# Small parameter loads on three DMA queues, the eleventh input-projection tile split earlier on ScalarE, and the latent norms moved ahead in a hybrid RG-LRU / MLA layer

## The chip, the cores and the metric

The kernel runs on one core of one Trainium2 chip. The metric is the device time of one execution in microseconds, and lower is better. TensorE (PE) does the matmuls, VectorE (DVE) and ScalarE (ACT) the elementwise work, GpSimd (POOL) some of it too, and SyncE (SP) only issues DMAs. ACT and POOL can issue DMAs as well.

## The reference

One layer with two kinds of sequences: a prompt of 512 tokens, and 8 sequences that decode one token each against 4096 cached tokens. So T = 520 columns pass through every projection.

```python
mod = jnp.dot(jax.nn.silu(c), lp['w_ada']) + lp['b_ada']
shift1, scale1, gate1, shift2, scale2, gate2 = jnp.split(mod[:, None, :], 6, axis=-1)
h = rms_norm(x, lp['norm1_g']) * (1.0 + scale1) + shift1
z = h @ lp['w_in']
x_lru, g_lru, q_lat, kv_lat, k_rope = jnp.split(z, IN_SPLITS, axis=-1)
x_conv, lru_buf_new = causal_dwconv(x_lru, ...)
hs, h_last = rg_lru(x_conv, pos, lru_h0, ...)          # h_t = a_t h_(t-1) + u_t, a = exp(log_a)
lru_out = hs * jax.nn.gelu(g_lru)
q = rms_norm(q_lat, lp['q_lora_norm_g']) @ lp['w_uq']   # then norms and rotary embedding
kv_lat = rms_norm(kv_lat, lp['kv_lora_norm_g'])
k_rope = apply_rope(rms_norm(k_rope, lp['k_rope_norm_g']), cos, sin)
attn = attend(q_nope, q_rope, kv_lat, k_rope)
mixed = concat(rms_norm(lru_out), rms_norm(attn)) @ lp['w_o']
x = x + gate1 * mixed
...                                                     # norm, up projection, convolution, gelu, down projection
```

All is fp32. A matmul of weight precision is done as three products of a high and a low part.

## The kernel before

Data lie transposed: 128 features on the partitions, 520 tokens in the free dimension. Each engine has its own program, written out by hand and run strictly in order; semaphores tie them together.

**The start.** SP loads constants, the conditions c, the prompt x in two halves of 1 MB, and then the chunks of `w_ada` (1 MB each, 24 in all) into a ring of four. Chunk 4 may only be loaded when PE has used chunk 0, and so on (`chunk_used`). ACT meanwhile issues 25 small loads: rows of parameters into `par_rows`, the states, and four copies of the page table into `page_of` (L1308 to L1326). Only then comes its first activation, the tanh behind silu(c) (L1329), from which DVE makes `cT` (L1681, L1682). PE turns c (J_C, PSUM buffer 0), then the eight tiles of x (J_XT), the fourth of which needs buffer 0 back from DVE. Then PE multiplies `cT` with the first two chunks of `w_ada` (L866), turns the parameter rows (it waits for all 21 loads counted by `s_par`), and goes on with chunks 2 and 3. The eight columns of shift and scale that come out of the first eight chunks are needed before the input projection can begin.

**The input projection.** `w_in` has 12 column tiles, taken in the order `WIN_ORDER`; `w_in(n)` is the n-th of them on PE (48 matmuls of 260 columns). Its weights pass through three stages: SP loads them, ACT rounds them to their high part (`in_high(n)`, L1342, which must wait until tile n - 2 is through PE, since `input_weights` has two buffers), and POOL makes the low part (`in_low(n)`, L732). Tiles 0 to 3 are the recurrent branch, 4 to 7 the latents of q, kv and the rotary key (`latent`, L1362), 8 to 11 the gate branch; the latter are copied out of PSUM on ACT by `gate_branch(0)` to `gate_branch(3)` (L1393). Between the tiles PE computes later chunks of `w_ada` (L866), turns their results (`mod_columns`), and makes the sums of squares for three norms (`nq`, `nkv`, `kr0`). Between the copies ACT computes the recurrence's coefficients: four Exp (L1385) and four Tanh (L1388), then two Ln (L1400, L1401) and an Exp (L1406), and the reciprocal roots of the three norms (`rstd`, L1297 and L1299). DVE does the scan (L1809) and multiplies the norms in (L1817, L1819, L1823).

**PSUM.** There are four buffers of two banks. Every piece of PE work has a number j and uses buffer j mod 4. It may start (`claim`) only when the piece with number j - 4 has been copied out. `IN_ORDER` is the list that gives the numbers in this stretch, and the programs of all engines follow them:

```python
def claim(eng, j, lap=0):
    if j // 4 >= 1 or not isinstance(lap, int):
        eng.wait_ge(psum_free[j % 4], j // 4 + lap)
```

After it come the small outputs of the recurrence, eight heads of prompt attention, the decode attention over the cache, and the MLP.

Of the kernel before, what the change touches and what calls it, by code (L numbers as in the profile page):

```python
# [111 lines left out]
class Steps:  # L112
# [20 lines left out]
    def leave(self, laps):  # L133
# [18 lines left out]
            + ["w6", "r4", "w7", "c3", "w8", "w9", "nq", "nkv", "kr0", "r5", "w10", "c4", "w11", "kr1", "c5"])  # L152
# [105 lines left out]
def build(nc, t):  # L258
    with ExitStack() as ctx:
# [308 lines left out]
        def _(sp):  # L568
# [30 lines left out]
            for c in range(8):  # L599
                if c >= 4:  # L600
                    chunk_used(sp, c - 4)
                modulation(c, c % 4, s_ada[c % 4])
                if c == 5:
                    w_in(0)
                    w_in(1)
# [226 lines left out]
        def _(pe):  # L832
# [135 lines left out]
            w_in(9)  # L968
# [8 lines left out]
            both(j, C("blk", QK, R)[:, NOPE:QK], sq[NOPE:QK, 3, :], True, True, R).then_inc(psum_full[j % 4], 1)  # L977
            later_chunk(12)
# [309 lines left out]
        def _(act):  # L1288
# [19 lines left out]
            for name in ("b_ada", "norm1_g", "lru_conv_b", "lru_b_a", "lru_b_x", "lru_lambda",  # L1308
                         "q_lora_norm_g", "kv_lora_norm_g", "lru_out_norm_g", "mla_out_norm_g", "norm2_g"):
                load_rows(name, t[name].rearrange("l (r p) -> (l r) p", p=P))  # L1310

            load_rows("lru_conv_w", t["lru_conv_w"].rearrange("l w (r p) -> (l w r) p", p=P))
            for name, a, b in (("gq", "q_nope_norm_g", "q_rope_norm_g"), ("gk", "k_nope_norm_g", "k_rope_norm_g")):
                r = ROWS[name]
                act.dma_start(par_rows[r:r + 1, 0, 0:NOPE], t[a]).then_inc(s_par, 16)
                act.dma_start(par_rows[r:r + 1, 0, NOPE:QK], t[b]).then_inc(s_par, 16)
            fw = t["ffn_conv_w"].rearrange("l w (r p) -> (l w r) p", p=P)
            act.dma_start(par_rows[0:4 * FT, 1, :], fw[0:4 * FT, :]).then_inc(s_par, 16)
            act.dma_start(par_rows[0:2 * FT, 2, :], fw[4 * FT:6 * FT, :]).then_inc(s_par, 16)
            act.dma_start(par_rows[2 * FT:4 * FT, 2, :],  # L1320
                         t["ffn_conv_b"].rearrange("l (r p) -> (l r) p", p=P)).then_inc(s_par, 16)
            act.dma_start(st_tok, t["state_lru_conv"].rearrange("l b r w -> (l b r) w")).then_inc(s_par, 16)
            act.dma_start(h0_tok, t["state_lru_h"].rearrange("l b w -> (l b) w")).then_inc(s_par, 16)

            for r in range(4):
                act.dma_start(page_of[r:P:4, :], t["page_table"].rearrange("b n -> n b"), allow_slow_non_contiguous=True).then_inc(s_pt, 16)  # L1326
# [55 lines left out]
            in_high(9)  # L1382

# [267 lines left out]
        def _(dve):  # L1651
# [163 lines left out]
            dve.wait_ge(s_rs, 2)  # L1815
            for k in range(2):
                V.scalar_tensor_tensor(qlT[:, k, :], qlT[:, k, :], pr("q_lora_norm_g", k), sq[:, 0, :], MUL, MUL).then_inc(s_ql, 1)  # L1817
            dve.wait_ge(s_rs, 3)
            V.scalar_tensor_tensor(kvT[:, :], kvT[:, :], pr("kv_lora_norm_g"), sq[:, 1, :], MUL, MUL).then_inc(s_kvn, 1)  # L1819
# [387 lines left out]
```

## Time and profile before

| | |
|---|---|
| median of 3 runs | 1120.18 us (1119.37 to 1123.1) |
| the profiled execution: its time | 1124.76 us |
| the profiled execution: its span in the trace | 1123.0 us |
| mean granted TensorE clock | 0.937 of full speed |
| PE busy | 1005.5 us, 90% of the span |
| DVE, ACT, POOL busy | 671.2, 537.9, 196.8 us |
| DMA | 100.28 MB, mean 89 GB/s |

PE is busy nine tenths of the span, and 70% of the chain that ended last is PE's. The 1.76 us between the span and the execution's time lie outside the trace. Everything in this case happens in the first 165 us: the start up to about 55 us, and the input projection up to about 150 us.

### The profile page before, as it was taken

What the parts mean: (1) busy time and instruction counts of PE and PEld (TensorE: products, weight loads), DVE (VectorE), ACT (ScalarE), POOL (GpSimd) and SP (SyncE); (2) the same over time, 40 slices, a digit from 0 to 9 for tenths busy, and PEclk for the clock granted to TensorE, in tenths of its full rate; (3) what the DMA queues carried; (4) which work ended last, traced back from release to release, by engine and by line L of the source; (5) the groups of instructions that cost most, each with busy time, mean ns of one, the idle gap of its engine ahead of it and who ended that gap; (6) DMA issues with size and microseconds to landing.
All of it is one profiled execution on the core that took longest, in us unless ns stands there. A gap on an engine that the chain in (4) does not pass through costs nothing.

```text
span 1123.0 us, 21332 instructions
## 1 busy us (share of the span) xinstructions
PE 1005.5 (90%) x7916; PEld 904.9 (81%) x7916; DVE 671.2 (60%) x1553; ACT 537.9 (48%) x875; POOL 196.8 (18%) x202
## 2 busy tenths in 40 slices
PE   6699989999797977978978699799999999999997
PEld 4388755444496977977878689699999999999997
DVE  4591356656676657567557545667777777753212
ACT  3314736555487758658658443344444434322210
POOL 0233231000123422432432202211000010100000
PEclk9699987988899999899899879899999999999999
DMA  8975534000100211211201014222423233263202
GB/s 292 303 244 180 187 117 156 13 10 2 49 18 20 95 50 45 93 34 60 92 21 56 1 38 132 51 76 75 112 75 110 77 94 93 81 177 91 71 3 77
DMA packets 110527, 100.28 MB, mean 89 GB/s; under 512 B 10451, under 2 KB 99454, under 8 KB 108381
## 3 DMA queue, kind: packets, MB, share of 16 engines
q1 hardware_dynamic: 105478, 78.36, 23.5%
q0 software_dynamic: 3456, 20.97, 5.3%
q8 instruction: 36, 0.59, 0.2%
q10 hardware_dynamic: 1539, 0.22, 0.1%
q14 instruction: 18, 0.15, 0.0%
HBM read 96.80 MB, written 2.94 MB: 89 GB/s over the span
## 4 chain that ended last, share of the span: by engine, by line
PE 70%; DVE 9%; ACT 8%; issue 8%; POOL 2%; DMA 1%; ACTq 1%; DVEq 0%; POOLq 0%; SPq 0%
PE ps L841 46%; PE ps L1174 12%; PE ps L836 4%; PE ps L1078 2%; PE ps L866 2%; POOL latents_low L795 2%; DMA RW<-w_ada 1%; PE ps L1134 1%; DVE RB L2009 1%; ACT RB L1528 1%; DVE RB L1893 1%; ACT RB L1512 1%; PE ps L1169 1%; PE ps L1042 1%; PE ps L1059 1%
## 5 line engine op out<-in xcount | busy, mean ns | idle before, releaser
L841 PE MATMUL ps<-normed_high,up_weights_high 128*128 128x260 f32 x704 | 142.7, 284 | 3.6 <-DVE normed_low L1728 3.4
L841 PE MATMUL ps<-normed_high,up_weights_low 128*128 128x260 f32 x704 | 142.3, 284 | 0.0
L841 PE MATMUL ps<-normed_low,up_weights_high 128*128 128x260 f32 x704 | 142.1, 284 | 0.0
L795 POOL TENSOR_TENSOR latents_low<-RB,latents_high 128x512 fp32r<-128x512 f32 (+1 forms) x72 | 86.1, 1202 | 274.6 <-ACT latents_high L1513 224.6
L1174 PE MATMUL ps<-key_weights_high,latents_high 128*128 128x260 f32 x528 | 120.7, 312 | 13.0 <-DVE RB L2007 11.8
L841 PEld LDWEIGHTS ps<-normed_high,up_weights_high 128*128 128x128 f32 x704 | 109.2, 190 | 4.3 <-issue 3.5
L1174 PE MATMUL ps<-key_weights_low,latents_high 128*128 128x260 f32 x528 | 111.4, 294 | 0.0
L1575 ACT ACTIVATE up_weights_high<-RW 128x1024 fp32r<-128x1024 f32 x44 | 46.6, 1060 | 135.4 <-PE ps L841 132.9
L1174 PE MATMUL ps<-key_weights_high,latents_low 128*128 128x260 f32 x528 | 111.3, 294 | 0.0
L841 PEld LDWEIGHTS ps<-normed_high,up_weights_low 128*128 128x128 f32 x704 | 109.0, 189 | 0.0
L841 PEld LDWEIGHTS ps<-normed_low,up_weights_high 128*128 128x128 f32 x704 | 108.8, 189 | 0.0
L1174 PEld LDWEIGHTS ps<-key_weights_high,latents_high 128*128 128x128 f32 x528 | 87.2, 204 | 16.7 <-DVE RB L2007 14.7
L1174 PEld LDWEIGHTS ps<-key_weights_high,latents_low 128*128 128x128 f32 x528 | 86.8, 201 | 0.0
L1174 PEld LDWEIGHTS ps<-key_weights_low,latents_high 128*128 128x128 f32 x528 | 86.8, 201 | 0.0
L2088 DVE TENSOR_TENSOR up_weights_low<-RW,up_weights_high 128x1024 fp32r<-128x1024 f32 x44 | 54.9, 1251 | 34.3 <-ACT up_weights_high L1575 29.9
L1528 ACT ACTIVATE qrot<-ps 128x512 f32<-128x512 f32 x88 | 52.9, 601 | 45.4 <-PE ps L1174 41.7
L841 PE MATMUL ps<-hidden_high,down_weights_high 128*128 128x260 f32 x352 | 71.4, 284 | 1.3 <-issue 1.3
L2006 DVE COPY RB<-ps 128x32 f32<-128x32 f32 (+1 forms) x72 | 13.6, 188 | 96.1 <-ACT qrot L1528 52.4
L841 PE MATMUL ps<-hidden_high,down_weights_low 128*128 128x260 f32 x352 | 70.8, 282 | 0.0
L841 PE MATMUL ps<-hidden_low,down_weights_high 128*128 128x260 f32 x352 | 70.7, 282 | 0.0
L2077 DVE TENSOR_TENSOR d<-ps,modT 128x8 f32<-128x8 f32 x16 | 2.7, 166 | 107.8 <-PE ps L841 107.8
L828 POOL COPY UT<-RW 128x10 f32 x44 | 24.8, 563 | 238.9 <-ACT RW L1601 238.9
(282 smaller groups left out, 2268.4 us busy)
## 6 DMA issues: line engine op xcount, KB each, us to landing
RW<-w_ada SPq DMA_DIRECT2D x24, 1024.0 KB, 7.9
RW<-w_up SPq DMA_DIRECT2D x44, 512.0 KB, 5.0
RW<-w_down SPq DMA_DIRECT2D x8, 1408.0 KB, 7.1
RW<-w_in SPq DMA_DIRECT2D x11, 512.0 KB, 8.3
RB<-w_o SPq DMA_DIRECT2D x8, 512.0 KB, 4.7
RB<-x_prompt SPq DMA_DIRECT2D x2, 1024.0 KB, 7.1
o_y_p<-RB SPq DMA_DIRECT2D x4, 512.0 KB
wuq<-w_uq SPq DMA_DIRECT2D x8, 96.0 KB, 2.1
```

Source lines behind the costliest of these rows:

```text
L795: nc.gpsimd.tensor_tensor(latL[:, g % 3, c:4 * P], turned[:, g % 3, c:4 * P], latH[:, g % 3, c:4 * P].bitcast(F32), ALU.subtract).then_inc ...
L828: nc.gpsimd.tensor_copy(UT[:, bass.ds(FT * g + 2 * i + e, 1), :], UU[e][:, g, NP:UW]).then_inc(s_ut, 1)
L836: return nc.tensor.transpose(out, in_, ident[0:n, 0:n])
L841: last = mm(ps[j % 4][rows[0]:rows[1], h, 0:H], lhsT, src[:, h * H:(h + 1) * H], start=start, stop=stop)
L866: last = mm(flat(j)[32 * g:32 * g + 32, 0:256], cT[:, k, :], ring[:, q if n < 2 else q % 2, kk, 256 * g:256 * g + 256], start=(k == 0), st ...
L1042: last = mm(flat(J.vw[e])[:, VD * a:VD * a + VD], kvT[:, P * a:P * a + P], wukv[:, e, NOPE:P], start=True, stop=True)
L1078: last = mm(flat(J.pv[e])[VD * e:VD * e + VD, P * a:NP], hb[e]["v"][:, VD * a:VD * a + VD], hb[e]["pt"][:, a, P * a:NP], start=(a == 0), s ...
L1174: last = mm(ps[j % 4][:, h, 0:KWW], a[:, g % 3, at:at + P], b[:, e, h, :], start=(i == 0), stop=(i == 2))
L1528: A(sqd[c % 3].rearrange("p (h n) -> p h n", h=2), ps[j % 4][:, :, 0:4 * NOPE], ACT.Square).then_inc(s_sqd, 1)
L1575: A(wuH[:, KT * g:KT * g + KT, :], wup[:, c, KT * g:KT * g + KT, :], ACT.Copy).then_inc(s_whi, 1)
L2006: V.tensor_copy(srd[e][:, HEADS * c:HEADS * c + w], flat(j)[:, KWW:KWW + w]).then_inc(s_snc, 1)
L2088: V.tensor_tensor(wuL[:, KT * g:KT * g + KT, :], wup[:, c, KT * g:KT * g + KT, :], wuH[:, KT * g:KT * g + KT, :].bitcast(F32), SUB).then_i ...
```

## The change

It has three parts. (1) Of ACT's 25 small loads six stay on ACT. Fifteen go to SP, behind the first four chunks of `w_ada` and ahead of the fifth. The four of the page table go to POOL. (2) `in_high(10)` on ACT moves ahead of the four Exp and four Tanh of the recurrence. (3) The sums of squares for the q, kv and rotary-key norms move ahead of `w_in(9)` on PE, their roots on ACT ahead of `gate_branch(0)`, and the two multiplications of q and kv on DVE ahead of the recurrence's tail; on DVE `mod_columns(3)` and `mod_rows(4)` move ahead of the wait for the Tanh. The job numbers follow by `IN_ORDER`.

```diff
-            + ["w6", "r4", "w7", "c3", "w8", "w9", "nq", "nkv", "kr0", "r5", "w10", "c4", "w11", "kr1", "c5"])
+            + ["w6", "r4", "w7", "c3", "w8", "nq", "nkv", "kr0", "w9", "r5", "w10", "c4", "w11", "kr1", "c5"])
...
-            for c in range(8):
-                if c >= 4:
-                    chunk_used(sp, c - 4)
+            for c in range(4):
+                modulation(c, c, s_ada[c])
+            sp.wait_ge(s_parz, 1)
...
+            for name in ("q_lora_norm_g", "kv_lora_norm_g", "lru_out_norm_g", "mla_out_norm_g", "norm2_g"):
+                load_rows(name, t[name].rearrange("l (r p) -> (l r) p", p=P))
...
+            sp.dma_start(h0_tok, t["state_lru_h"].rearrange("l b w -> (l b) w")).then_inc(s_par, 16)
+
+            for c in range(4, 8):
+                chunk_used(sp, c - 4)
                 modulation(c, c % 4, s_ada[c % 4])
...
             nc.gpsimd.memset(BD[:, :, :, :], 0.0).then_inc(s_bdz, 1)
+            for r in range(4):
+                nc.gpsimd.dma_start(page_of[r:P:4, :], t["page_table"].rearrange("b n -> n b"), allow_slow_non_contiguous=True).then_inc(s_pt, 16)
...
             w_in(8)
             later_chunk(11)
-            w_in(9)
             norm_sum(J_NQ, 2, KT)
             norm_sum(J_NKV, 1, KT + 2, 2)
...
+            w_in(9)
             later_chunk(12)
...
             latent(11, krT[NOPE:QK, :])
             in_high(9)
+            in_high(10)
 
             for k in range(LT):
                 v = st.did(A(AA[:, k, :], TA[:, k, :], ACT.Exp, bias=small[:, 32 + k:33 + k], scale=small[:, 32 + k:33 + k]))
...
             nc.scalar.preload_act_table_set("natural_log_exp_and_others")
+            rstd(J_NQ, QL, dst=sq[:, 0, :]).then_inc(s_rs, 1)
+            rstd(J_NKV, KV, dst=sq[:, 1, :]).then_inc(s_rs, 1)
+            rstd(J_KR[0], 1, (NOPE, QK), dst=sq[NOPE:QK, 2, :]).then_inc(s_rs, 1)
             gate_branch(0)
-            in_high(10)
...
+            mod_columns(3)
+            mod_rows(4)
             dve.wait_ge(s_ta, 4)
             V.tensor_scalar(TA[:, :, :], TA[:, :, :], 1e-18, None, ALU.max).then_inc(s_tiny, 1)
-            mod_columns(3)
-            mod_rows(4)
+            dve.wait_ge(s_rs, 2)
+            for k in range(2):
+                V.scalar_tensor_tensor(qlT[:, k, :], qlT[:, k, :], pr("q_lora_norm_g", k), sq[:, 0, :], MUL, MUL).then_inc(s_ql, 1)
```

On ACT, before, from `in_high(9)` on, which follows the copy of the last latent tile; L1385 and L1388 are the Exp and Tanh of the recurrence, L1393 is `gate_branch`, L1342 is `in_high`:

```order
L1342 ACTIVATE input_weights_high<-RW 128x1024 [waits psum_full0,w_in_in0]
L1385 ACTIVATE RB<-RB,small 128x520 x4
L1388 ACTIVATE RB<-RB,small 128x520 [waits act_steps]
L1388 ACTIVATE RB<-RB,small 128x520 x3
L1395 ACT_TABLE_LOAD
L1393 ACTIVATE RB<-ps 128x520 [waits psum_full2]
L1342 ACTIVATE input_weights_high<-RW 128x1024 [waits psum_full2,w_in_in1]
```

And now, from `in_high(10)` on, which follows `in_high(9)` directly (line numbers are those of the changed kernel: L1349 is `in_high`, L1393 and L1396 are Exp and Tanh, L1321 and L1323 the roots of the norms, L1401 `gate_branch`):

```order
L1349 ACTIVATE input_weights_high<-RW 128x1024 [waits psum_full2,w_in_in1]
L1393 ACTIVATE RB<-RB,small 128x520 x4
L1396 ACTIVATE RB<-RB,small 128x520 [waits act_steps]
L1396 ACTIVATE RB<-RB,small 128x520 x3
L1403 ACT_TABLE_LOAD
L1321 ACTIVATE sq<-ps,small 128x520 [waits psum_full3]
L1323 ACTIVATE sq<-sq 128x520 [waits psum_free3]
L1321 ACTIVATE sq<-ps,small 128x520 [waits psum_full0]
L1323 ACTIVATE sq<-sq 128x520 [waits psum_free0]
L1321 ACTIVATE sq<-ps,small 32x520 [waits psum_full1]
L1323 ACTIVATE sq<-sq 32x520 [waits psum_free1]
L1401 ACTIVATE RB<-ps 128x520 [waits psum_full2]
```

The L1349 of tile 10, which waits for tile 8 to be through PE (`psum_full2`), now stands ahead of the eight Exp and Tanh, and six operations of the norms stand between the table load and the copy of tile 8.

On PE, before, from the last matmuls of tile 8 (buffer `ps2`) to the first of tile 9:

```order
L841 MATMUL ps2<-normed_high_59,input_weights_low_65 128x260 x2
L866 MATMUL ps3<-RW,cT 32x256 [waits w_ada_second_in1]
L866 MATMUL ps3<-RW,cT 32x256 x7
L841 MATMUL ps3<-normed_high_59,input_weights_high_64 128x260 [waits input_weights_low,psum_free3]
L841 MATMUL ps3<-normed_high_59,input_weights_high_64 128x260
```

And now:

```order
L865 MATMUL ps2<-normed_high_59,input_weights_low_65 128x260 x2
L890 MATMUL ps3<-RW,cT 32x256 [waits w_ada_second_in1]
L890 MATMUL ps3<-RW,cT 32x256 x7
L865 MATMUL ps3<-sq,cst 128x260 [waits squares_done,psum_free3]
L865 MATMUL ps3<-sq,cst 128x260
L865 MATMUL ps3<-sq,cst 128x260 [waits squares_done]
L865 MATMUL ps3<-sq,cst 128x260
L865 MATMUL ps0<-sq,cst 128x260 [waits squares_done,psum_free0]
L865 MATMUL ps0<-sq,cst 128x260
L865 MATMUL ps1<-sq,cst 32x260 [waits squares_done,psum_free1,other_consts_in]
L865 MATMUL ps1<-sq,cst 32x260
L865 MATMUL ps2<-normed_high_59,input_weights_high_64 128x260 [waits input_weights_low,psum_free2]
```

The norms' sums take buffers 3, 0 and 1, and tile 9 now takes buffer 2, which is tile 8's; before it took buffer 3, that of the `w_ada` row ahead of it.

## Rows read from the trace of the kernel before

**Rows 1.** The page: shares of the chain of work that ended last.

```profile
PE 70%; DVE 9%; ACT 8%; issue 8%; POOL 2%; DMA 1%; ACTq 1%; DVEq 0%; POOLq 0%; SPq 0%
```

**Rows 2.** The chain of waits, first 60 us: start, duration, engine and line.

```profile
12.27 1.28 ACT L1329
...
22.51 6.30 DMA RW<-w_ada
```

**Rows 3.** The timeline of PE and ACT in the first 24 us.

```profile
4.40 0.99 PE L836 MATMUL ps<-cst,RB 9*128 9x9 f32 x8 [4.40 <-DMA RB<-x_sample]
8.17 3.81 PE L836 MATMUL ps<-cst,RB 128*128 128x128 f32 x15 [2.78 <-DMA RB<-x_prompt]
14.48 6.30 PE L836 MATMUL ps<-cst,RB 128*128 128x128 f32 x25 [2.50 <-DVE cT L1682]
20.71 2.60 PE L866 MATMUL ps<-RW,cT 128*32 128x256 f32 x32
...
3.64 0.38 ACTq L1306 DMA_DIRECT2D par_rows<-q_lora_norm_g  x1
...
9.19 0.32 ACTq L1323 DMA_DIRECT2D RB<-state_lru_h  x1
```

**Rows 4.** DMA queues and rate in the first 60 us (40 slices of 1.5 us).

```profile
GB/s 0 139 124 393 396 401 392 403 378 386 318 391 383 323 45 63 284 369 363 358 335 298 374 401 415 421 377 323 376 415 407 291 195 273 267 62 0 0 87 330
...
q10 hardware_dynamic: 1539, 0.22, 2.4%
```

**Rows 5.** Timelines: SP's issues of transfers, POOL's first split, DVE's reading of the page table.

```profile
4.61 1.50 SPq L583 DMA_DIRECT2D RW<-w_ada  x2
...
27.43 4.28 SPq L583 DMA_DIRECT2D RW<-w_ada  x2
...
34.45 4.66 POOL L732 TENSOR_TENSOR input_weights_low<-RW,input_weights_high 128x1024 fp32r<-128x1024 f32 x2 [32.41 <-ACT input_weights_high L1342]
...
93.83 0.22 DVE L1788 TENSOR_SCALAR row_of<-page_of,cst 128x8 int32<-128x8 int32 x1
```

**Rows 6.** PE's timeline around tiles 8 and 9 and the norms' sums.

```profile
122.85 0.40 PE L841 MATMUL ps<-normed_high,input_weights_low 128*128 128x260 f32 x2
123.18 1.07 PE L866 MATMUL ps<-RW,cT 128*32 128x256 f32 x16
124.99 0.51 PE L841 MATMUL ps<-normed_high,input_weights_high 128*128 128x260 f32 x2 [0.74 <-DVE newrow L1664]
...
130.85 3.78 PE L841 MATMUL ps<-sq,cst 128*128 128x260 f32 x16
134.56 1.93 PE L866 MATMUL ps<-RW,cT 128*32 128x256 f32 x32
```

**Rows 7.** ACT's timeline in the same stretch.

```profile
116.19 1.06 ACT L1342 ACTIVATE input_weights_high<-RW 128x1024 fp32r<-128x1024 f32 x1
117.15 2.95 ACT L1385 ACTIVATE RB<-RB,small 128x520 f32<-128x520 f32 x4
...
123.11 1.28 ACT L1395 ACT_TABLE_LOAD   x1
124.41 0.60 ACT L1393 ACTIVATE RB<-ps 128x520 f32<-128x520 f32 x1
...
134.32 0.69 ACT L1297 ACTIVATE sq<-ps,small 128x520 f32<-128x520 f32 x1
...
137.68 0.63 ACT L1299 ACTIVATE sq<-sq 32x520 f32<-32x520 f32 x1
```

**Rows 8.** DVE's timeline: its wait for the last `w_ada` row.

```profile
150.70 0.42 DVE L1664 COPY newrow<-ps 128x256 f32<-128x256 f32 x1 [5.32 <-PE ps L866]
```

**Rows 9.** PE's timeline after a wait of 5.14 us, in the decode attention.

```profile
407.67 0.53 PE L1169 MATMUL ps<-QBD,RB 128*128 x2 [5.14 <-POOL latents_low L795]
408.02 0.78 PE L1174 MATMUL ps<-key_weights_high,latents_high 128*128 128x260 f32 x2
...
411.20 0.42 PE L1174 MATMUL ps<-key_weights_low,latents_high 128*128 128x260 f32 x2
```

More of the change, by code:

```diff
@@ L597, in w_in, with load_rows @@
                 sp.dma_start(RA[:, n % 3, :, at:at + w], wi[:, :, P * m:P * m + w]).then_inc(s_win[n % 3], 16)
-            for c in range(8):
-                if c >= 4:
-                    chunk_used(sp, c - 4)
+            for c in range(4):
+                modulation(c, c, s_ada[c])
+            sp.wait_ge(s_parz, 1)
+            def load_rows(name, src):
+                n = src.shape[0]
+                sp.dma_start(par_rows[ROWS[name]:ROWS[name] + n, 0, 0:src.shape[1]], src).then_inc(s_par, 16)
+            for name in ("q_lora_norm_g", "kv_lora_norm_g", "lru_out_norm_g", "mla_out_norm_g", "norm2_g"):
+                load_rows(name, t[name].rearrange("l (r p) -> (l r) p", p=P))
+            load_rows("lru_conv_w", t["lru_conv_w"].rearrange("l w (r p) -> (l w r) p", p=P))
+            for name, a, b in (("gq", "q_nope_norm_g", "q_rope_norm_g"), ("gk", "k_nope_norm_g", "k_rope_norm_g")):
+                r = ROWS[name]
+                sp.dma_start(par_rows[r:r + 1, 0, 0:NOPE], t[a]).then_inc(s_par, 16)
+                sp.dma_start(par_rows[r:r + 1, 0, NOPE:QK], t[b]).then_inc(s_par, 16)
+            fw = t["ffn_conv_w"].rearrange("l w (r p) -> (l w r) p", p=P)
+            sp.dma_start(par_rows[0:4 * FT, 1, :], fw[0:4 * FT, :]).then_inc(s_par, 16)
+            sp.dma_start(par_rows[0:2 * FT, 2, :], fw[4 * FT:6 * FT, :]).then_inc(s_par, 16)
+            sp.dma_start(par_rows[2 * FT:4 * FT, 2, :],
+                         t["ffn_conv_b"].rearrange("l (r p) -> (l r) p", p=P)).then_inc(s_par, 16)
+            sp.dma_start(st_tok, t["state_lru_conv"].rearrange("l b r w -> (l b r) w")).then_inc(s_par, 16)
+            sp.dma_start(h0_tok, t["state_lru_h"].rearrange("l b w -> (l b) w")).then_inc(s_par, 16)
+            for c in range(4, 8):
+                chunk_used(sp, c - 4)
                 modulation(c, c % 4, s_ada[c % 4])
@@ L1306, in load_rows @@
                 act.dma_start(par_rows[ROWS[name]:ROWS[name] + n, part, 0:src.shape[1]], src).then_inc(s_par, 16)
-            for name in ("b_ada", "norm1_g", "lru_conv_b", "lru_b_a", "lru_b_x", "lru_lambda",
-                         "q_lora_norm_g", "kv_lora_norm_g", "lru_out_norm_g", "mla_out_norm_g", "norm2_g"):
+            for name in ("b_ada", "norm1_g", "lru_conv_b", "lru_b_a", "lru_b_x", "lru_lambda"):
                 load_rows(name, t[name].rearrange("l (r p) -> (l r) p", p=P))
[L1312 to L1326, printed above, removed]
             full(act, J_C)
@@ L1406, in _ @@
             A(TA[:, :, :], TA[:, :, :], ACT.Exp, scale=0.5).then_inc(s_lru, 1)
-            rstd(J_NQ, QL, dst=sq[:, 0, :]).then_inc(s_rs, 1)
-            rstd(J_NKV, KV, dst=sq[:, 1, :]).then_inc(s_rs, 1)
-            rstd(J_KR[0], 1, (NOPE, QK), dst=sq[NOPE:QK, 2, :]).then_inc(s_rs, 1)
             gate_branch(2)
@@ L1797, in _ @@
             v = st.did(V.scalar_tensor_tensor(TI[:, :, :], TI[:, :, :], 1.0, XC[:, :, :], ADD, MUL))
+            mod_columns(3)
+            mod_rows(4)
             dve.wait_ge(s_ta, 4)
             V.tensor_scalar(TA[:, :, :], TA[:, :, :], 1e-18, None, ALU.max).then_inc(s_tiny, 1)
-            mod_columns(3)
-            mod_rows(4)
+            dve.wait_ge(s_rs, 2)
+            for k in range(2):
+                V.scalar_tensor_tensor(qlT[:, k, :], qlT[:, k, :], pr("q_lora_norm_g", k), sq[:, 0, :], MUL, MUL).then_inc(s_ql, 1)
+            dve.wait_ge(s_rs, 3)
+            V.scalar_tensor_tensor(kvT[:, :], kvT[:, :], pr("kv_lora_norm_g"), sq[:, 1, :], MUL, MUL).then_inc(s_kvn, 1)
             dve.wait_ge(s_lru, 1)
@@ L1813, in _ @@
             dve.wait_ge(s_lrud, 1)
[L1815 to L1819, printed above, removed]
             dve.wait_ge(s_rs, 4)
```

## The prediction

> **What bounds the kernel now.** I read the page first: the chain that ended last is 70% PE [rows 1], so a change pays where PE waits. Then the chain of waits over the first 60 us, the timelines of PE, ACT and SP beside it and the DMA rates by slice, for the small loads. Then PE's, ACT's and DVE's timelines from 115 to 155 us, for the other two parts, and last a place in the decode stage where PE works after a long wait, for the clock.
>
> At the start ACT issues loads until its first table load at 12.27 us [rows 2], and PE, which had turned the first three tiles of x by 11.98, waits 2.50 us for what DVE makes of ACT's tanh [rows 3]. PE then reaches the first `w_ada` chunk at 20.71 us, and only when that is used does SP issue chunk 4, at 22.51. In between the DMA engines run dry: 45 and 63 GB/s in the two slices from 21 to 24 us, between slices of 323 and 284 [rows 4]. From there the chain runs through DMA: the load issued at 22.51 takes 6.30 us to land [rows 2]. So this stage goes as early as chunk 4 is issued.
>
> In the input projection PE is the bound. Tile 8 ends at 122.85 + 0.40 = 123.25 us, and tile 9 starts at 124.99 after a wait of only 0.74 [rows 6]. ACT uses exactly the time in which PE does tile 8 for the recurrence: Exp and Tanh from 117.15 until the table load at 123.11, and at 124.41 it copies tile 8 out [rows 7]. That ordering is what the change touches.
>
> **Part 1, the small loads.** ACT's sixth load is issued before the seventh begins at 3.64 us, and the turned c is ready at 4.40 + 0.99 = 5.39 [rows 3]. With the table load of 1.28 us [rows 2] done by 4.9, the tanh can run at about 5.4 and `cT` is there before 6.5, so PE isn't stopped: 3.81 + 6.30 = 10.11 us of turning from 8.17 ends at 18.28 in place of 20.71 [rows 3]. That is 2.43 us. The second half of x and chunk 0 have to be there: at the rates of rows 4, the 2.3 MB of constants, c and x have passed by about 9.3 us, chunk 0 by about 12, and chunk 3 by about 20.4. Chunk 4 is then issued at about 20.1, and the dry stretch shrinks by as much. All that follows in this stage keeps its distance to chunk 4, until PE-bound work begins at about 55 us. Gain: 2.4 us.
>
> What the moved loads cost: fifteen issues on SP, 0.39 us each if they are like ACT's (3.64 to 9.19 + 0.32 = 9.51, fifteen issues [rows 3]), begin at 4.61 + 1.50 = 6.1 us, when chunk 3 has been issued [rows 5], and end at about 12, well before 20.1; SP is waiting there anyway. They stand ahead of chunk 4 in SP's queue. All 1539 packets of ACT's queue, of which the page table is 1024, took 2.4% of 60 us, 1.4 us [rows 4]; so the delay of chunk 4 is between 0 and 1.4 us, and nearer to 0, since it falls into what remains of the dry stretch. The page table is read at 93.83 us; on POOL its four issues stand in front of nothing until 34.45 [rows 5]. Bounds for part 1: gain 1.0 to 2.4.
>
> **Parts 2 and 3, on ACT and PE.** These must be costed together, since the price comes from PSUM. `w_in(9)` now takes tile 8's buffer, which `gate_branch(0)` frees. So tile 9 can't start before ACT has copied tile 8, and ACT has put everything else first. From tile 8's end at 123.25, in the times of before [rows 7]:
>
> - `in_high(10)`: it waits for that end itself. 1.06 us
> - four Exp, four Tanh: they stood under tile 8, and now start after it. From 116.19 + 1.06 = 117.25 to 123.11: 5.86 us
> - table load with its gap, 123.11 to 124.41: 1.30 us
> - three norm roots, from 134.32 to 137.68 + 0.63 = 138.31: 3.99 us
> - the copy of tile 8: 0.60 us
>
> The sum is 12.81 us, and tile 9 starts at 136.1 in place of 124.99, 11.1 later. The norms' sums have meanwhile been done, from about 124.8 (chunk 11 ends at 124.25, and DVE copies a row in 0.42 [rows 8]). Between tile 9 and chunk 12 they took 134.56 - 130.85 = 3.71 us [rows 6]. Net: 11.1 - 3.7 = 7.4 us later, in which PE has nothing at all to do from about 128.5 to 136.1.
>
> Is any of it hidden further on? The moved multiplications on DVE give nothing: DVE had finished its work at 145.4 and sat idle for 5.32 us before 150.70, waiting for PE [rows 8]. Nor do they hold anything up: with the Exp and Tanh 7 us late, Ln, Ln, Exp and the scan follow, and by their durations before, DVE is through with `krT` about 3 us before it is needed. The later tiles keep their distances. The earlier split of tile 10 gives nothing either: in_low(10) had no one waiting for it. From 151 us on the chain passes from PE to DVE, ACT and POOL without a reserve that could absorb a delay.
>
> **The clock.** After a wait of 5.14 us PE's pairs of matmuls from 408.02 to 411.20 took 3.18 us for seven steps [rows 9], where tile 9 makes its 24 steps in 130.85 - 124.99 = 5.86 us, 0.244 each [rows 6], so 1.71 for seven. The new wait is longer, 7.6 us, with little work on either side of it left out. I take the same loss: 1.5 us. Bounds: 0 (PE keeps its higher level, 2.4 GHz) and 1.5.
>
> **The sum.** -2.4 + 7.4 + 1.5 = +6.5 us. Against the profiled execution, 1124.76 us, that is 1131.3. That execution stands 4.6 us above the median of the runs, 1120.18; the predicted median is 1126.7.
>
> **The rivals.**
> 1. *The start gives nothing, or costs* (0.14). SP's queue accepts only so much ahead: two `w_ada` issues that began at 27.43 took 4.28 us [rows 5], when much was outstanding. If the fifteen small loads are held until chunk 3 is through at 20.4, their 5.9 us of issuing push chunk 4 from 20.1 to 26.3, 3.8 us later than before. Or the parameters land late: PE needs them at about 21 us, before chunk 2. No row of before shows when they land. If they come with chunk 3 plus one transfer's latency, at 22 to 23 us, PE loses 1 to 2 us there, but chunk 6, which waits for chunk 2, was issued only from 27.43 [rows 5], so about 2 us of cover remain. The result is between +8.9 (no gain) and +12.7 us: 1129 to 1133. Against it: before, SP had issued x and four chunks by 6.1 us without such a delay [rows 5].
> 2. *The wait is partly absorbed* (0.10). If the clock stays up and ACT's list is shorter than I count, because the roots of the norms start only with their sums or the pipelined Exp overlap more, the loss is 5 us and the net +2 to +3: 1122 to 1123.5, within the measurement. For it speaks only that neighbouring ACT instructions overlap by 0.1 us (116.19 + 1.06 against 117.15 [rows 7]).
> 3. *Faster* (0.06). Tile 9 is not held by tile 8's copy, because ACT reaches it in time: then only the start's 2.4 us and tile 9's 0.74 us remain, 1117.0. This case decides when the copy ends before 124.99 + 3.71 + 2.4 = 131.1 us in before's times, that is when ACT's list of 12.8 us takes under 7.8. The eight Exp and Tanh alone are 5.9 of it, and the two waits on buffer 2 are in the program's order; so its chance is small. It is also the case where the change's second part does not reach the path.
>
> **How the numbers follow.** Forecast 0.70, with a range of its own of 1124 to 1129 (clock loss 0 to 1.5, start 1.0 to 2.4, and a median of three that varies by 1 to 2 us). Rival 1 takes 0.14, rival 2 0.10, rival 3 0.06. The range of 1123 to 1131 holds the forecast's and parts of rivals 1 and 2. A difference of 0.3%, 3.4 us, is about what a measurement of this kernel can tell from none. The forecast and rival 1 are slower by more, 0.84, and a little of rival 2; most of rival 2 and half of rival 3 lie within it, half of rival 3 below.
>
> **What would show it.** PE's first table-dependent wait (2.50 us for `cT`) gone, chunk 0 on PE at 18.3 us, chunk 4 issued at about 20.1, and tile 0 starting about 2.4 us earlier. Then PE idle for about 7.6 us in front of the first matmul of `w_in(9)`, put down to ACT's copy (L1401), ACT idle from about 115 to 121 us and full after that, and some 3 us of matmuls at the lower granted clock behind it. The end of tile 11 some 6.5 us later. I am wrong if that wait is short, if the parameters hold PE for more than 2 us, or if the stages after 165 us change by more than 1 us.

## The result, and the profile of the changed kernel

| | median | single runs |
|---|---|---|
| changed kernel | 1131.11 us | 1126.37 to 1136.23, 9 runs |
| kernel before, in turn with it | 1123.1 us | 1119.37 to 1126.61, 9 runs |
| ratio | 1.0073 | 95% interval 1.0045 to 1.0101 |
| profiled execution: its time and span | 1130.16 and 1128.4 us | clock 0.936 |

The change makes the kernel slower by 8.0 us. The forecast was slower, 1126.7 us, in a range of 1123 to 1131; the median lies 0.1 us above that range. The kernel before also stands 2.9 us above the median that the forecast started from: its nine runs contain the three of that median and six more.

The chain of work on the page of the changed kernel, against [rows 1]: PE's share fell from 70% to 68%, and DMA's rose from 1% to 2%.

```profile
PE 68%; DVE 10%; ACT 9%; issue 8%; POOL 2%; DMA 2%; SPq 1%; ACTq 0%; DVEq 0%; POOLq 0%
```

PE's timeline from the start, against [rows 3] (start, duration, engine and line, operation, count, and in brackets the idle time with what ended it):

```profile
8.04 10.04 PE L860 MATMUL ps<-cst,RB 128*128 128x128 f32 x40 [2.47 <-DMA RB<-x_prompt]
18.01 3.63 PE L890 MATMUL ps<-RW,cT 128*32 128x256 f32 x32
25.15 0.71 PE L860 MATMUL ps<-cst,par_rows 109*128 109x109 f32 x3 [3.51 <-DMA RB<-state_lru_h]
...
...
38.49 1.93 PE L890 MATMUL ps<-RW,cT 128*32 128x256 f32 x16 [0.61 <-DMA RW<-w_ada]
41.29 0.66 PE L860 MATMUL ps<-cst,newrow 128*128 128x128 f32 x2 [0.86 <-DVE newrow L1671]
```

The last two rows are chunk 7, the last that the input projection waits for, and what PE does with the row that DVE copies from it. In the kernel before they read:

```profile
40.21 1.93 PE L866 MATMUL ps<-RW,cT 128*32 128x256 f32 x16 [0.62 <-DMA RW<-w_ada]
42.78 0.66 PE L836 MATMUL ps<-cst,newrow 128*128 128x128 f32 x2 [0.64 <-DVE newrow L1664]
```

The wait of 2.50 us for `cT` is gone. A wait of 3.51 us for the last small load, `state_lru_h`, stands 7 us later. SP's timeline shows where that load stands, and that chunk 4 goes out at 20.00 us, where before had 22.51:

```profile
3.21 2.92 SPq L583 DMA_DIRECT2D RW<-w_ada  x4
6.18 1.53 SPq L605 DMA_DIRECT2D par_rows<-q_lora_norm_g  x1
...
14.17 0.58 SPq L620 DMA_DIRECT2D RB<-state_lru_h  x1
20.00 2.10 SPq L583 DMA_DIRECT2D RW<-w_ada  x2
```

In the chain of waits it takes 10.84 us from issue to landing, behind the four chunks of 1 MB, and DVE's products with `rs`, which follow the late norm sum, are on the chain with 9.21 us:

```profile
14.17 10.84 DMA RB<-state_lru_h
...
30.06 0.70 ACT rs L1321
30.79 0.65 ACT rs L1323
31.46 9.21 DVE RB L1714 x8
...
40.81 0.35 DVE newrow L1671
```

In the kernel before the same eight products took 4.91 us:

```profile
28.08 4.91 DVE L1707 TENSOR_TENSOR RB<-xT,rs 128x512 f32<-128x512 f32 x8 [0.17 <-ACT rs L1299]
```

The rates of the first 60 us, against [rows 4], in slices of 1.5 us: the dry stretch of 45 and 63 GB/s is gone, and a hollow of 264, 260 and 139 GB/s stands at 6 to 10.5 us, after POOL's four page-table issues at 2.00 us. GpSimd's queue is the third row.

```profile
GB/s 0 120 134 398 264 260 139 414 418 421 410 415 407 404 340 320 377 393 373 308 307 394 410 405 433 352 330 394 407 408 228 204 240 262 51 0 0 79 319 382
...
q0 software_dynamic: 128, 0.00, 2.0%
```

PE's timeline of the input projection, against [rows 6]: the norm sums at 122.99 us, then 7.47 us of nothing until ACT frees tile 8's buffer.

```profile
121.31 1.07 PE L890 MATMUL ps<-RW,cT 128*32 128x256 f32 x16
122.99 3.89 PE L865 MATMUL ps<-sq,cst 128*128 128x260 f32 x16 [0.62 <-DVE newrow L1671]
134.34 0.80 PE L865 MATMUL ps<-normed_high,input_weights_high 128*128 128x260 f32 x2 [7.47 <-ACT RB L1401]
...
141.72 1.93 PE L890 MATMUL ps<-RW,cT 128*32 128x256 f32 x32
...
158.36 1.06 PE L865 MATMUL ps<-krT,cst 32*32 32x260 f32 x4 [0.61 <-DVE newrow L1671]
```

And ACT's, against [rows 7]:

```profile
121.47 1.06 ACT L1349 ACTIVATE input_weights_high<-RW 128x1024 fp32r<-128x1024 f32 x1 [5.72 <-PE ps L865]
122.44 2.94 ACT L1393 ACTIVATE RB<-RB,small 128x520 f32<-128x520 f32 x4
125.41 2.95 ACT L1396 ACTIVATE RB<-RB,small 128x520 f32<-128x520 f32 x4
128.38 1.28 ACT L1403 ACT_TABLE_LOAD   x1
129.68 0.69 ACT L1321 ACTIVATE sq<-ps,small 128x520 f32<-128x520 f32 x1
...
133.69 0.60 ACT L1401 ACTIVATE RB<-ps 128x520 f32<-128x520 f32 x1
```

To compare kernels I use three places that every trace has (times in us): the first chunk pair behind tile 0 ("start"), tile 9, and the norm sum of the recurrence's output ("165 us"). What is left of the span is the last column.

| profiled execution | start | tile 9 (wait) | 165 us | rest | span |
|---|---|---|---|---|---|
| before | 55.70 | 124.99 (0.74) | 162.52 | 960.5 | 1123.0 |
| changed | 54.22 | 134.34 (7.47) | 169.69 | 958.7 | 1128.4 |
| e1, loads alone | 55.42 | 124.71 (1.32) | 162.23 | 955.7 | 1117.9 |
| e2, no loads | 54.58 | 134.58 (7.46) | 170.20 | 960.1 | 1130.3 |
| e3, split back | 54.23 | 129.90 (2.85) | 165.31 | 964.4 | 1129.7 |
| e4, split alone | 55.58 | 131.14 (7.88) | 170.34 | 956.5 | 1126.8 |
| e5, page table alone | 54.52 | 123.86 (1.50) | 161.40 | 960.0 | 1121.4 |
| e6, copy first | 55.27 | 127.82 (none) | 161.75 | 955.8 | 1117.5 |
| e7, rows turned later | 53.54 | 123.08 (1.02) | 160.60 | 959.9 | 1120.5 |
| e8, page table later | 51.41 | 120.70 (1.86) | 158.22 | 959.9 | 1118.1 |
| e9, e3 again | 54.97 | 130.40 (2.84) | 164.34 | 952.6 | 1116.9 |
| e10, e8 and rows ahead | 52.16 | 120.48 (0.62) | 157.99 | 959.7 | 1117.7 |

In the profiled pair the changed kernel is 7.17 us behind at 165 us and 5.4 us behind at the end.

### The profile page after: what moved, and what is told of

Same layout as the page of the kernel before. It is cut to its first block, busy times and chain, and to the rows that moved or that the text cites. A ratio compares the mean times of both kernels' runs of the same rounds, so it can differ in the third digit from the quotient of the medians.

```text
span 1128.4 us, 21332 instructions
## 1 busy us (share of the span) xinstructions
PE 1004.8 (89%) x7916; PEld 904.3 (80%) x7916; DVE 676.0 (60%) x1553; ACT 538.1 (48%) x875; POOL 200.3 (18%) x206
## 4 chain that ended last, share of the span: by engine, by line
PE 68%; DVE 10%; ACT 9%; issue 8%; POOL 2%; DMA 2%; SPq 1%; ACTq 0%; DVEq 0%; POOLq 0%
PE ps L865 45%; PE ps L1198 12%; PE ps L860 3%; PE ps L1102 2%; POOL latents_low L819 2%; PE ps L890 1%; DVE RB L2016 1%; DVE RB L1900 1%; PE ps L1158 1%; ACT RB L1535 1%; ACT RB L1519 1%; DMA RB<-state_lru_h 1%; PE ps L1193 1%; DVE RB L1714 1%; ACT latents_high L1520 1%
```

## The experiments

The theory after the result: all of the loss is the order on ACT (parts 2 and 3), and the start gives little, since the small loads arrive late. The rival: the loads themselves cost something, or the stages behind 165 us do.

### e1 and e2: the loads alone, and all but the loads

e1 is the kernel before with the diff's SP, POOL and ACT load lines alone, e2 the changed kernel without them.

> Part 1 of the change alone (small loads on three queues), input projection as before. In the changed kernel's trace the start is 1.6 us earlier than before, not 2.4. Theory: the loads gain 1.6 us, all of it in the first 55 us, and everything after keeps the distance: span some 1.6 us shorter than before, with PE's wait for the last parameter row (3.5 us) in it. Rival: that wait costs more than it seems, and the loads are part of the loss: no gain, or slower by 1 us or more.

> Parts 2 and 3 of the change without part 1. Theory: the start as before, then 7.3 us of delay in front of tile 9 and 1.5 us at the lower clock: +8.8 us. Rival (parts interact, since the delay of ACT depends on when loads arrive): another distance than the change's +7.2 plus 1.6.

e1: 1121.6 us in 10 runs against 1122.58, ratio 0.9998, 0.9969 to 1.0027. e2: 1132.05 us in 9 runs against 1121.36, ratio 1.0081, 1.0058 to 1.0103. The loads alone change nothing that can be measured, and the other two parts carry the loss: 9.1 us by the ratio. At 165 us e2 is 7.7 us behind before, and e1 0.3 ahead, which add up to the change's own 7.2 within 0.3 us, so the parts don't interact much. The 1.6 us that e1's theory wanted aren't there.

e1's start takes the same course as the changed kernel's, though it ends 1.2 us later. PE waited 4.19 us for `state_lru_h`, until 25.39. Its chain has the late load and DVE's products with `rs`, as the changed kernel's has:

```profile
14.71 10.54 DMA RB<-state_lru_h
...
32.66 9.21 DVE RB L1714 x8
```

### e7: the parameter rows turned later

e1 with this edit on PE, which takes the rows' late landing off the norm sum (the turning of the parameter rows stands where the dots are):

```diff
+            first_chunk(0, 2)
+            first_chunk(0, 3)
+            claim(pe, J_N1)
+            pe.wait_ge(s_n1, KT - 1)
+            both(J_N1, ones, sq[:, 0, :], True, True).then_inc(psum_full[J_N1 % 4], 1)
...
-            first_chunk(0, 2)
-            first_chunk(0, 3)
-            claim(pe, J_N1)
-            pe.wait_ge(s_n1, KT - 1)
-            both(J_N1, ones, sq[:, 0, :], True, True).then_inc(psum_full[J_N1 % 4], 1)
```

> Part 1 alone, but PE turns the parameter rows after chunks 2 and 3 and the first norm's sum, so that the late parameters don't hold those up. Theory: the lateness was covered but for 0.1 to 0.2 us: start 1.6 to 1.8 us earlier than before. Rival: it was the lateness that cost, through the norm's root and DVE's eight products beside POOL's split: 2.4 us.

1120.54 us in 12 runs, ratio 0.9988, 0.9966 to 1.001. DVE's products with `rs`, in the trace of e7:

```profile
28.56 4.90 DVE L1714 TENSOR_TENSOR RB<-xT,rs 128x512 f32<-128x512 f32 x8
```

POOL's split of the first two `w_in` tiles ran from 32.81 us there, with the products nearly through at 33.46. In the changed kernel the products began at 31.46 and the split at 32.74:

```profile
32.74 5.57 POOL L756 TENSOR_TENSOR input_weights_low<-RW,input_weights_high 128x1024 fp32r<-128x1024 f32 x2 [28.11 <-ACT input_weights_high L1349]
```

So the same eight products take 4.90 us alone and 9.21 beside the split. The start stands at 53.54 us, 1.9 earlier than in e1 and 1.3 earlier than the mean of the five traces with the changed start (54.82). Starts of one and the same code spread by 1.2 us, so one trace says no more than that some 1.3 to 1.9 us of what the start term lacked are here; the median, 1120.54 us, is not clear of before's. It speaks for the rival's mechanism and against the theory, by which the lateness was covered. The edit takes two things away at once, the wait for the rows ahead of the norm sum and the meeting of DVE and POOL; the products' own 4.3 us are more than the whole gain, since chunk 7 sets the time once they are early.

### e5 and e8: only the page table moved

e5 is the kernel before with the page table's four loads on POOL. In e8 they stay on ACT but stand behind the eight scalings of `h` in its program. The expectation puts them at about 48 us; the trace has them from 39.91 to 42.62 us, while ACT is at the first of the scalings:

```diff
-            for r in range(4):
-                act.dma_start(page_of[r:P:4, :], t["page_table"].rearrange("b n -> n b"), allow_slow_non_contiguous=True).then_inc(s_pt, 16)
             full(act, J_C)
...
+            for r in range(4):
+                act.dma_start(page_of[r:P:4, :], t["page_table"].rearrange("b n -> n b"), allow_slow_non_contiguous=True).then_inc(s_pt, 16)
             act.wait_ge(s_sp, 1)
```

> The kernel before with the page table's four loads on POOL and all other small loads left on ACT. ACT then reaches its table load at 9.5 us, early enough for PE. Theory: the gain of the start is limited by the DMA stream, which POOL's page table loads slow to 264, 260 and 139 GB/s in three slices from 6 to 10.5 us; the fifteen loads on SP have no part in it: gain 1.6 us as in the change. Rival: the late parameters (or their packets ahead of chunk 4) took the missing 0.8 us: gain 2.4 us here.

> The kernel before with the page table's four loads issued on ACT at about 48 us (behind the eight scalings of h) in place of ahead of its first activation; all other loads as before. Theory: PE's wait for cT goes as in the change, and the table's 1024 small packets leave the stream that bounds the start: 2.4 us gained, up to 3 if their packets cost the stream something there. Rival: the start is bounded by something else at 1.6.

e5: 1121.1 us in 12 runs, ratio 0.9997, 0.9969 to 1.0024. Its start stands at 54.52 us, 1.2 earlier than before's, less than the theory's 1.6 and the rival's 2.4. ACT's table load begins at 11.06 us there and not at 9.5, since its other issues took longer, and PE still waits 1.45 us for `cT`; the hollow in the DMA rates is there too (last section). Which of the two takes how much was not tried. e8: 1120.13 us in 12 runs, ratio 0.9984, 0.9961 to 1.0006. e8's start on PE:

```profile
7.74 8.48 PE L836 MATMUL ps<-cst,RB 128*128 128x128 f32 x40 [2.34 <-DMA RB<-x_prompt]
16.15 1.93 PE L866 MATMUL ps<-RW,cT 128*32 128x256 f32 x32
18.06 0.31 PE L836 MATMUL ps<-cst,par_rows 109*128 109x109 f32 x1
```

No wait for `cT`, none for the parameters, and no hollow in the DMA rates:

```profile
GB/s 0 138 125 388 402 390 408 385 388 380 361 404 410 412 412 407 396 323 293 318 402 410 418 416 328 346 412 404 379 188 211 269 193 25 0 46 289 393 415 378
```

The start stands at 51.41 us, 4.3 earlier than before, and above the theory's 2.4 to 3. Some of that is the execution's own: the 40 matmuls took 8.48 us here, and 10.05 in e10, which loads in the same way and starts 3.5 us earlier than before. In both, taking only the page table out of ACT's queue ahead of the tanh was enough to end the wait for `cT`; the whole time of e8 is not clear of before's. Moving fifteen more loads behind `w_ada` on SP made the parameters late.

### e4, e3, e9: the split alone, and the split back

e4 is the kernel before with the first edit below. e3 and e9 are one kernel, the changed one with it undone.

```diff
             in_high(9)
+            in_high(10)
...
             gate_branch(0)
-            in_high(10)
```

> The kernel before with in_high(10) alone moved ahead of Exp and Tanh. Theory: Exp and Tanh start only after tile 8; tile 9 here uses another buffer, but that is freed by DVE's mod_rows(4), which stands behind DVE's wait for the Tanh: tile 9 starts about 7.2 us later than before, some 1.5 us at the lower clock follow, net +8.5 to +9. Rival: without the reordered norms nothing waits for the Exp, and the net is under +2.

> The changed kernel with in_high(10) back behind gate_branch(0), so that Exp and Tanh lie under tile 8 again; norms ahead of tile 9 as in the change. Theory (the price is ACT's list between tile 8's end and its copy): the list is now table load, three roots from about 2 us after the sums begin, copy; tile 9 starts 6.4 to 6.6 us after before's, of which 3.7 are the sums moved ahead: 2.7 us lost, PE idle under 3 us and no stretch at the lower clock, with the start's 1.6 gained a net of +1. Rival (the reordered norms and the shared buffer are the price, the split has no waiter): the wait stays near 7.5 us and the net near +7.

> The changed kernel with the split of tile 10 back behind the first gate tile, once more and with more runs. Its profiled execution was only 2.8 us behind the one of before at 165 us, yet four runs gave 1132.57 us against 1122.58. Theory (the rest of the difference is the clock in prompt attention, which drops at other moments from one execution to the next, and four runs drew badly): over many runs the median is 1122 to 1128 us, and the single times spread over 8 us or more. Rival (the clock's drops in prompt attention follow from how the input stage ended, here three roots ahead of the copy and a wait of 2.85 us before tile 9, and come in every execution): the median stays at 1131 to 1134 us with a spread under 5 us, and the segment from the norm sum of the recurrence's output to the key stage is again about 134 us in the profile.

e4: 1130.97 us in 10 runs, ratio 1.0085, 1.0059 to 1.0111, and 7.8 us behind at 165 us, as its theory has it. So one line on ACT has the price of parts 2 and 3 together. In the order of before, tile 9 takes the buffer of a `w_ada` row, which DVE empties behind its wait for the Tanh. DVE's timeline of e4:

```profile
129.28 1.24 DVE L1799 TENSOR_SCALAR RB<-RB 128x2080 f32<-128x2080 f32 x1 [24.84 <-ACT RB L1389]
130.44 0.29 DVE L1672 TENSOR_TENSOR modT<-ps,par 128x36 f32<-128x36 f32 x2
130.66 0.42 DVE L1664 COPY newrow<-ps 128x256 f32<-128x256 f32 x1
```

It is another buffer than the prediction's, held by the same Exp and Tanh. They had run under tile 8; now they wait for tile 8's end, because `in_high(10)` ahead of them does.

e3: tile 9's wait falls from 7.47 to 2.85 us, as the theory has it and not the rival, and at 165 us it is 2.8 behind before. Against the theory there was a stretch at the lower clock: tile 9 took 7.47 us. Yet its time was 1132.57 us in 4 runs, ratio 1.0102, 1.0049 to 1.0155. e9, the same kernel with 12 runs, gave 1129.69 us, ratio 1.0063, 1.0035 to 1.0092. Its single times fall into two groups:

```
1118.66 1120.76 1121.91 | 1128.84 1129.33 1129.44 1129.94 1130.60 1131.82 1132.20 1133.50 1133.78
```

Neither expectation of e9 held whole: the spread of 15 us is the theory's, but the median is above its 1122 to 1128; the median is also under the rival's 1131 to 1134, and the spread is not its 5 us. The profiled executions of e3 and e9 came from different groups, which shows where the 12 us lie. At 165 us they are 1.0 us apart, by tile 9: behind a wait of 2.84 us it took 136.36 - 130.40 = 5.96 us in e9, at full clock, and 7.47 in e3. Windows within tile 9 (busy time and instructions of PE, weight loads, DVE, ACT, POOL; granted clock; DMA share, GB/s), e3's from 131.3 us and all of e9's:

```profile
131.30:134.30 3.00, 3.00 (x15) 3.00 (x15) 0.00 (x0) 3.00 (x2) 2.08 (x1) 0.50 0.00 0
...
130.40:136.30 5.90, 5.90 (x48) 5.82 (x48) 1.13 (x1) 4.69 (x3) 2.42 (x1) 1.00 0.00 0
```

The rest of the difference comes later: PE's matmuls behind the wait of 2.36 us for DVE, in prompt attention, start at 299.46 us in e3 and at 288.14 in e9. The windows of that stretch, with the columns as above, first e3:

```profile
214.00:234.00 20.00, 19.20 (x71) 10.15 (x71) 12.31 (x41) 10.40 (x27) 0.00 (x0) 0.85 0.07 16
234.00:254.00 20.00, 18.01 (x59) 8.33 (x58) 11.19 (x24) 7.98 (x15) 0.00 (x0) 0.74 0.00 0
254.00:274.00 20.00, 18.89 (x80) 10.50 (x80) 12.36 (x39) 14.62 (x34) 0.00 (x0) 1.00 0.06 16
274.00:288.00 14.00, 12.32 (x36) 5.43 (x35) 8.64 (x19) 3.17 (x6) 0.00 (x0) 0.64 0.00 1
```

and e9:

```profile
214.00:234.00 20.00, 18.90 (x81) 10.54 (x80) 12.96 (x43) 14.38 (x34) 0.00 (x0) 1.00 0.07 16
234.00:254.00 20.00, 17.53 (x78) 9.56 (x77) 15.04 (x42) 9.90 (x23) 0.00 (x0) 1.00 0.06 16
254.00:274.00 20.00, 18.03 (x66) 8.70 (x65) 14.52 (x35) 11.20 (x22) 0.00 (x0) 0.86 0.00 0
274.00:288.00 14.00, 11.02 (x47) 5.92 (x45) 7.95 (x31) 7.73 (x20) 0.00 (x0) 0.95 0.00 1
```

One kernel, the same instructions: PE stays at full clock from 214 to 254 us in e9, and drops twice in that time in e3 (0.85 and 0.74 as means over a window, so part of each at the lower level). The time that the drops take is (1.00 - 0.85 + 1.00 - 0.74) x 20 = 8.2 us in the first two windows and 0.36 x 14 - 0.05 x 14 = 4.3 in the last, less 0.14 x 20 = 2.8 in the third: 9.7 us, of the 10.3 that came in between 165 us and that wait.

From the norm sum at 165 us to the matmuls behind that wait it is 134.15 us in e3 and 123.80 in e9. Of the other ten traces two have the short form as well (123.65 in e1, 123.71 in e6), e4 has 126.25, and seven have 129.4 to 130.4, the kernel before with 130.40 and the changed one with 129.43 among them. So this stage has no part in the 7.17 us between the profiled pair, and e3 is the only trace with the longest form.

### e6: the copy of tile 8 ahead of the roots

The changed kernel, with `gate_branch(0)` and `in_high(10)` ahead of the three norm roots (the Exp and Tanh stand where the dots are):

```diff
-            in_high(10)
...
+            gate_branch(0)
+            in_high(10)
             rstd(J_NQ, QL, dst=sq[:, 0, :]).then_inc(s_rs, 1)
             rstd(J_NKV, KV, dst=sq[:, 1, :]).then_inc(s_rs, 1)
             rstd(J_KR[0], 1, (NOPE, QK), dst=sq[NOPE:QK, 2, :]).then_inc(s_rs, 1)
-            gate_branch(0)
```

> The changed kernel with in_high(10) back and the copy of tile 8 ahead of the three roots on ACT; the sums stay ahead of tile 9 on PE. Theory: the copy is done at about the time the sums are through, so PE doesn't wait for it, and the order of the norms costs nothing: net -1.6 to -2 against before (the start's gain, and the wait for newrow of 0.7 us gone in part). Rival: sharing tile 8's buffer costs in itself, with a wait of 1 us or more in front of tile 9.

1121.54 us in 10 runs, ratio 1.0003, 0.9976 to 1.003. ACT has the Exp and Tanh under tile 8 again and copies tile 8 at once:

```profile
119.71 2.96 ACT L1395 ACTIVATE RB<-RB,small 128x520 f32<-128x520 f32 x4
122.69 1.28 ACT L1402 ACT_TABLE_LOAD   x1
123.98 0.60 ACT L1400 ACTIVATE RB<-ps 128x520 f32<-128x520 f32 x1
```

The whole loss is gone, with the loads and the norm sums as the change has them, and PE doesn't wait in front of tile 9. The rival's wait of 1 us or more did not come; the theory's gain of 1.6 to 2 us isn't seen in the median either. Of the change's moves only the two on ACT cost: `in_high(10)` ahead of the Exp, and the roots ahead of the copy.

### e10: the page table later, and DVE's rows ahead of its wait

e8 with this edit on DVE:

```diff
+            mod_columns(3)
+            mod_rows(4)
             dve.wait_ge(s_ta, 4)
             V.tensor_scalar(TA[:, :, :], TA[:, :, :], 1e-18, None, ALU.max).then_inc(s_tiny, 1)
-            mod_columns(3)
-            mod_rows(4)
```

> The kernel before with two moves: the four page-table loads issued on ScalarE's queue behind the eight scalings of h (at about 48 us), and on VectorE the columns of chunk 3 and the rows of chunk 4 taken ahead of its wait for the recurrence's Tanh. Theory: the first move starts the chunks of w_ada about 4.5 us earlier on TensorE and brings the norm sum of the recurrence's output 4.3 us forward as it did alone; the second takes the wait of 1.86 us for newrow before tile 9 down to about 0.6, so the norm sum stands at 156.5 to 157.5 us where before had 162.52, and the median is 1114 to 1119 us against 1121.5 to 1123. Rival A (VectorE's place is not what holds newrow, the chunk's own arrival is): the wait stays at 1.8 us and the norm sum at 158.2. Rival B (what the start wins is lost again by the clock behind 165 us): the norm sum is early but the median is 1120 to 1123 us.

1119.55 us in 12 runs (1113.22 to 1123.4) against 1122.45, ratio 0.9976, 0.9956 to 0.9997. PE's timeline shows the wait at 0.62 us, as the theory has it, where e8 had 1.86:

```profile
120.48 0.50 PE L841 MATMUL ps<-normed_high,input_weights_high 128*128 128x260 f32 x2 [0.62 <-DVE newrow L1663]
```

At 165 us it stands at 157.99, between the theory's 156.5 to 157.5 and rival A's 158.2; its start is 0.75 us later than e8's, by the 40 matmuls, and the shorter wait makes up for that. Of the 4.5 us won at 165 us, 2.9 are seen in the median. The median lies between the theory's 1119 and rival B's 1120, so some of what is won seems to be lost behind 165 us. It is the fastest version in this study, 0.24% faster than before, though its interval ends at 0.9997: of ten versions tried one can come out so by chance.

## Why the prediction was wrong, point by point

The direction and the main mechanism were right. The forecast missed by 4.4 us: 2.9 lie in the base, the median from which it started, and 1.5 in the difference, 8.0 us for the sum's 6.5. In the sum the step that failed is the gain at the start, put at 2.4 us, of which the traces show 1.5 in the profiled pair and 0.5 on the mean. The assumption that the later stages keep their time failed too, at a small price here.

**The base.** The forecast stood on a median of three runs, 1120.18 us. With six more runs, in turn with the changed kernel, it is 1123.1, and later turns gave 1122.58 (25 runs), 1121.36 (34) and 1122.45 (23). The prediction allowed 1 to 2 us for this; it was 2.9. It took the profiled execution (1124.76) as 4.6 us off the median; against these medians it is 1.7 to 3.4 off. With 1123.1 as the base, the sum of +6.5 would have given 1129.6.

**"Gain: 2.4 us" at the start.** This step failed in size. Its first events came true one by one: the wait for `cT` is gone, chunk 0 starts at 18.01 us (forecast 18.3), chunk 4 is issued at 20.00 (20.1). "All that follows in this stage keeps its distance to chunk 4" is the sentence that failed. e3 shows it best: there chunk 4 was issued 3.4 us earlier than in the changed kernel's trace, and the start stands at the same 54.2 us.

```profile
16.64 2.34 SPq L583 DMA_DIRECT2D RW<-w_ada  x2
```

Two things took the gain away. Both begin with the parameter rows, which landed at 25.0 us. First, chunk 7 came only 1.7 us earlier than before (38.49 for 40.21 in the profiled pair; on the mean of the five traces with the changed start against the three with the old one 38.24 for 39.79, or 1.5). Chunks 6 and 7 may be issued when PE has used chunks 2 and 3, and these stand behind the rows on PE: SP issued them from 27.78 us on, where before had 27.43. What holds chunk 7 beyond that is not shown. e7 issues them at 26.20 us and has chunk 7 no earlier than 38.32; e8 issues them at 22.97, has no hollow in its DMA stream, and has chunk 7 at 36.48. Second, the first norm sum stands behind the rows on PE as well. That put DVE's products beside POOL's split, and they took 9.21 us for 4.91, so that the last row came late: PE waited for it 0.86, 2.42, 1.28, 2.15 and 1.86 us behind chunk 7 in the five traces (changed, e1, e3, e6, e9), and 0.64 in each of the three others. That is 1.1 us on the mean, but only 0.2 in the changed kernel's own trace. What remained was 1.48 us in the profiled pair, and 0.5 in the mean over the five (54.22, 55.42, 54.23, 55.27, 54.97) against the three (55.70, 54.58, 55.58).

The first rival had the kind of event right, and its reason, 4 MB ahead on the same queue. It put the landing at 22 to 23 us and the loss at PE at 1 to 2; measured were 25.0 and 3.51, which is over the 2 us that the prediction named as a sign of being wrong. By the rule of the Trainium skill that each DMA engine consumes a ring in order ("DMA: Bandwidth & Descriptors", "Queues, rings and completion order") the small loads wait behind those 4 MB; the trace agrees, with 10.84 us from the issue of the last to its landing. The rival took the 2 us of cover for chunk 6 as enough and did not follow the norm sum. Its median, 1129 to 1133, holds the result, but partly by luck, because the base was low: it has no gain at the start and up to 3.8 us of loss, and neither came. Its other branch, SP's queue held up until chunk 3 is through, did not come: the fifteen issues took 8.6 us and not 5.9, but ended at 14.75 us, well before chunk 4.

**"12.81 us", ACT's list before the copy of tile 8.** Right. From tile 8's end, when `in_high(10)` starts at 121.47, to the end of the copy at 134.29 are 12.82 us, and the wait was 7.47 (forecast 7.6). Tile 9 is 9.35 us later than before, or 10.8 without the profiled pair's start; the forecast had 11.1. e4 adds that the copy's buffer is only one of two ways to pay this: in the order of before DVE's row would have held tile 9 as long. The root is `in_high(10)` ahead of the Exp, and e6 takes the cost away.

**"3.71" for the norm sums.** Right: 3.89 us at 122.99, gone from behind tile 9.

**The clock, "1.5 us".** Right. Tile 9 took 141.72 - 134.34 = 7.38 us in place of 5.86, with a granted clock of 0.50 in its first 3.16 us and 1.00 from 137.6 us on. The two other traces with a wait of this length show it too (7.68 us in e2, 7.54 in e4). But e3 shows the same loss, 137.37 - 129.90 = 7.47 us for tile 9, behind a wait of only 2.85 us, and e9, the same kernel behind the same wait, shows next to none (5.96). So the size of the loss did not go with the length of the wait, and behind the shorter wait it came in one execution of two. Parts 2 and 3 come to 7.18 + 1.48 = 8.7 us at tile 11's end (158.36 against 151.18), where the forecast had 8.9. The second and third rival did not come.

**"if the stages after 165 us change by more than 1 us".** They did; small in the sum. The rest of the span is 1.8 us shorter in the changed kernel's profile and spreads from 952.6 to 964.4 us over the twelve traces. Two of these are one kernel, 11.8 us apart, 10.3 of it in prompt attention, nearly all by the clock's drops. The changed kernel's own profile has that stage no longer than before's. What stays open: whether a late start into that stage makes the long form more likely. For it speaks that e3 and e9 are only 1.8 to 2.8 us behind at 165 us, but have 13 of their 16 runs in the upper group, and e9's ratio makes 7.1 us; that e2 and e4 lose 9.1 and 9.5 us by their ratios for 7.7 and 7.8 at 165 us; and that e8 and e10 show 1.8 and 2.7 us by their ratios of the 4.3 and 4.5 that they win there. What selects the group in a run was not tried.

## What to carry to other kernels

An instruction that waits for a tile's end, moved ahead of work that ran under that tile, puts the whole of that work behind the tile, and here it cost 7.8 us for one line moved: look at what the engine did during the tile, and at every buffer whose release stands behind it, on other engines too. A small load can take as long as what stands ahead of it in its queue (10.84 us for 16 KB here); take only the slow ones out of the way of the first needed work, and ask of each moved one who reads it first. Where the same program spreads over 10 us, take the base from many runs and compare traces at a fixed place in the program, not by their spans.

## What the runs showed of the hardware

- DVE's 128x512 products took 4.90 us for eight by themselves and 9.21 us when POOL's two 128x1024 subtractions ran beside them (9.21 or 9.22 in all five traces with the changed start). They were not all slower by the same: in the changed kernel's trace their median is 0.69 us and the longest took 2.84, about one of POOL's. POOL's two took 4.66 us alone and 5.25 to 5.57 then.
- Four page-table loads of 1 KB each, issued by POOL, held up the other queue's stream. e5 moves nothing else, and has 263, 192 and 190 GB/s in three slices of 1.5 us where before had 396, 401 and 392:

```profile
GB/s 0 141 151 362 263 192 190 411 418 399 375 340 416 407 352 257 369 303 369 338 317 316 399 407 414 432 336 336 398 412 389 218 227 285 179 20 0 52 279 385
...
q0 software_dynamic: 128, 0.00, 2.3%
```

  That is (396 + 401 + 392 - 263 - 192 - 190) x 1.5 us = 0.8 MB, or 2 us of the stream at 400 GB/s, for 128 packets. e2, with the table on ACT, has no such hollow. On ACT's queue the table made 1539 - 451 = 1088 packets, and took 2.70 us of ACT's issuing time instead.
- Behind waits of 7.46 to 7.88 us tile 9 took 7.38 to 7.68 us, where it took 5.86 before. Behind one of 2.85 us it took 7.47 in one execution of a kernel, with a granted clock of 0.50 for 3 us, and 5.96 in another, at full clock. In the same two executions the clock in prompt attention dropped at 214 to 254 us in the first and stayed full until 254 in the second, and that stage took 10 us of 1120 more in the first.
